# Sink heads: q produced in turned form, cosine and sine parts stacked to 128 rows of contraction

## The reference, cut to what matters

```python
def apply_rope(x, cos, sin):
    x1, x2 = jnp.split(xf, 2, axis=-1)
    return jnp.concatenate([x1 * c - x2 * s, x2 * c + x1 * s], axis=-1)

qa = apply_rope(qa.reshape(B, S, A_HEADS, A_HEAD_DIM), cos_a, sin_a)
ka = apply_rope(ka.reshape(B, S, A_KV_HEADS, A_HEAD_DIM), cos_a, sin_a)
y_a = swa_sink_attention(qa, ka, va, sinks)   # softmax(q k^T / 8, sink) v, bands of 2 chunks of 64 tokens
```

## Time and profile before

| | |
|---|---|
| runs | 763.81, 763.9, 764.29 us |
| profiled execution | 763.82 us, its span 762.1 us |
| granted TensorE clock | 0.998 of full |
| TensorE busy | 747.8 us, 98% of the span, 3970 matmuls |
| VectorE, ScalarE, GpSimd busy | 512.4, 417.0, 164.7 us |
| chain that ended last | TensorE 90%, VectorE 6%, ScalarE 2% |

### The profile page before, as it was taken

How to read it: one execution, slowest core, us unless ns; L and a number is a source line. 1 busy time by engine, 2 the same in 40 slices (tenths; PEclk the granted TensorE clock), 3 DMA queues, 4 the chain that set the end, 5 groups by cost and what they waited for, 6 DMA issues and landing times.

```text
span 762.1 us, 10863 instructions
## 1 busy us (share of the span) xinstructions
PE 747.8 (98%) x3970; PEld 631.5 (83%) x3970; DVE 512.4 (67%) x674; ACT 417.0 (55%) x789; POOL 164.7 (22%) x250
## 2 busy tenths in 40 slices
PE   6999999999999999999999999999999999999996
PEld 5978887888798888888888888788888988888885
DVE  5789867667765666656686887685568656565664
ACT  6847675534564444444577676654348444544452
POOL 1966422100131111100125443220002210111110
PEclk9999999999999999999999999999999999999999
DMA  7739533455465555566337493335463656564521
GB/s 256 254 99 299 186 111 111 151 182 171 158 201 186 193 193 171 163 216 207 104 103 257 174 304 111 111 111 168 164 220 111 221 166 221 176 209 171 202 68 55
DMA packets 68619, 132.16 MB, mean 173 GB/s; under 512 B 2874, under 2 KB 10596, under 8 KB 68324
## 3 DMA queue, kind: packets, MB, share of 16 engines
q1 hardware_dynamic: 68308, 131.64, 52.1%
q10 hardware_dynamic: 272, 0.00, 0.0%
HBM read 130.59 MB, written 1.05 MB: 173 GB/s over the span
## 4 chain that ended last, share of the span: by engine, by line
PE 90%; DVE 6%; ACT 2%; issue 1%; DMA 1%; POOL 0%; SPq 0%; POOLq 0%; ACTq 0%; DVEq 0%
PE acc L1353 18%; PE acc L1355 17%; PE acc L1354 17%; PE tp L1640 6%; PE sc L1640 6%; PE tp L1328 4%; PE sc L1435 3%; PE acc L1387 3%; PE tp L1642 3%; PE sc L1642 3%; DVE w_lo L995 2%; PE sc L1353 1%; PE sc L1354 1%; PE sc L1355 1%; DVE x L1160 1%; PE sc L1626 1%
## 5 line engine op out<-in xcount | busy, mean ns | idle before, releaser
L995 DVE TENSOR_TENSOR w_lo<-raw,w_hi 128x1024 fp32r<-128x1024 f32 (+3 forms) x256 | 307.9, 1222 | 163.0 <-ACT w_hi L654 161.4
L654 ACT CAST w_hi<-raw 128x1024 fp32r<-128x1024 f32 (+3 forms) x256 | 251.3, 996 | 181.1 <-PE acc L1355 107.9
L1353 PE MATMUL acc<-w_hi,s_hi 128*128 128x512 f32 (+1 forms) x328 | 127.7, 389 | 0.0
L1355 PE MATMUL acc<-w_hi,s_lo 128*128 128x512 f32 (+1 forms) x328 | 126.6, 386 | 0.0
L1354 PE MATMUL acc<-w_lo,s_hi 128*128 128x512 f32 (+1 forms) x328 | 126.5, 386 | 0.0
L1353 PE MATMUL acc<-w_hi,s_both 128*128 128x512 f32 (+2 forms) x320 | 122.0, 381 | 1.0 <-DVE w_lo L995 0.6
L1355 PE MATMUL acc<-w_hi,s_both 128*128 128x512 f32 (+2 forms) x320 | 118.5, 370 | 0.0
L1354 PE MATMUL acc<-w_lo,s_both 128*128 128x512 f32 (+2 forms) x320 | 118.4, 370 | 0.0
L517 POOL TENSOR_TENSOR tok<-k_b 128x512 f32<-128x512 f32 x32 | 36.9, 1159 | 266.0 <-ACT k_b L750 244.7
L1353 PEld LDWEIGHTS acc<-w_hi,s_hi 128*128 128x128 f32 x328 | 61.6, 188 | 13.1 <-DVE w_lo L995 1.3
L1355 PEld LDWEIGHTS acc<-w_hi,s_lo 128*128 128x128 f32 x328 | 61.6, 188 | 12.3
(11 more groups left out here) (186 smaller groups left out, 1076.0 us busy)
## 6 DMA issues: line engine op xcount, KB each, us to landing
raw<-in_w_mlp_in SPq DMA_DIRECT2D x32, 1024.0 KB, 5.4
raw<-in_w_mlp_out SPq DMA_DIRECT2D x32, 1024.0 KB, 5.0
raw<-in_w_in SPq DMA_DIRECT2D x24, 1024.0 KB, 5.4
raw<-in_w_oa SPq DMA_DIRECT2D x8, 1024.0 KB, 5.0
raw<-in_w_out SPq DMA_DIRECT2D x8, 1024.0 KB, 4.9
raw<-in_w_ob SPq DMA_DIRECT2D x4, 1024.0 KB, 5.0
raw<-in_w_in SPq DMA_DIRECT2D x3, 768.0 KB, 4.8
raw<-in_w_in SPq DMA_DIRECT2D x4, 576.0 KB, 6.5
```

Of the source, the lines that this page charges most:

```text
L654: s.copy(split_view(w_hi, p), raw_view(p)).then_inc(hi_ready, 1)
L995: v.tensor_tensor(split_view(w_lo, p), raw_view(p), split_view(w_hi, p).bitcast(F32), ALU.subtract)\
L1353: mm(banks[t][:, 0:N], h[:, kk, tk], wh[:, k, :], start=(start and k == 0), stop=False)
L1355: ins = mm(banks[t][:, 0:N], low[:, kk, tk], wh[:, k, :], start=False, stop=(stop and k == b - a - 1))
```

## The change

1. q of A comes out turned. A new `turned_product` (the former `mlp_in` with the banks as an argument) takes the weights as the stationary operand and the activations `s1` of all 256 tokens as the moving one: 24 matmuls of 256 columns for each piece in place of 12 of 512. Each bank then holds two blocks of [128 columns of q, 256 tokens].
2. The rotation is moved into the scores. For a head, q . rope = [q cos ; q sin] against [k' ; k' with its halves exchanged, one negated]. `qT_a` gets 128 rows: 64 of q times cosine, 64 of q times sine; `kT_a` gets 128 rows in two orders, for even and odd heads. The eight instructions for each group (`multiply_q`, four for each bank, 64 rows x 512 elements, PSUM times a table) are VectorE's.
3. The table is cosine and sine times 1/rms of the token (`scaled_cs`, four 128x128 instructions on GpSimd), turned by TensorE (new fill "angles", four blocks, ahead of "ckv") and copied by ScalarE (`turned_cs`, 128x512).
4. The products that next overwrite the banks of q now wait for VectorE: uq0 for `multiply_q` of group 0, uq1 for that of group 1, bank by bank (`q_taken`).
5. Gone: ScalarE's four copies of q to `tok`, the rotations of q on VectorE and GpSimd, the four turnings "qA" with their copies, GpSimd's clearing of the two extra rows. k of A is turned in one fill of four blocks (k' and the exchanged k') in place of two of one block, and copied by three instructions in place of four; GpSimd makes the exchanged halves with two small instructions for each token tile.

```diff
+            def multiply_q(pos, c, u):
+                src = acc[2 * (1 - c) + u][:, :].rearrange("p (x c q) -> p x c q", x=2, c=NCHUNK)
+                for odd in range(2):
+                    rows = slice(odd * AD, (odd + 1) * AD)
+                    for a in range(2):
+                        to = slice((a + odd) % 2 * AD, ((a + odd) % 2 + 1) * AD)
+                        table = turned_cs[rows, a]...to_broadcast([AD, 2, NCHUNK, CHUNK])
+                        ins = v.tensor_tensor(qT_a[to, c, :, odd, u]..., src[rows], table, ALU.mult)
+                ins.then_inc(q_multiplied, 1)
...
 # VectorE, behind lo(18), the key latent and neg_sink
-                dve.wait_ge(tables_ready, 1)
-                for c, p in ((0, 18), (1, 22)):
-                    lo(pos, p)
-                    dve.wait_ge(proj_out, pos.count(14, 2 * PROJ[f"q{c}"] + 1))
-                    rope(v, ..., between=lambda: lo(pos, p + 1)).then_inc(roped, 1)
-                    dve.wait_ge(roped, pos.count(2, c + 1))
-                lo(pos, 25)
-                turned(pos, ("qA", 0, 0))
-                lo(pos, 27)
-                turned(pos, ("qA", 0, 1))
+                dve.wait_ge(bank_done(("angles",)), bank_turn(pos, ("angles",)))
+                for c, p in ((0, 15), (1, 19)):
+                    lo(pos, p + 3)
+                    used(pos, p)
+                    multiply_q(pos, c, 0)
+                    lo(pos, p + 4)
+                    multiply_q(pos, c, 1)
...
 # TensorE
-                for i, p in enumerate(range(12, 16)):
-                    product(pos, p, 4 * (i // 2), s1, pair[1], i == 0, i == 3, free=latent_free(1) if i == 0 else None)
+                turned_product(pos, 12, pair[1], free=latent_free(1))
+                pe.wait_ge(angle_rows, pos.count(1, 1))
+                turn(pos, ("angles",), [scaled_cs[:, a, t]... for a in range(2) for t in range(TT)])
                 turn(pos, ("ckv",), ...)
-                for i, p in enumerate(range(16, 20)):
-                    product(pos, p, 4 * (i // 2), s1, pair[0], i == 0, i == 3, free=projected(pos, "kv") if i == 0 else None)
+                turned_product(pos, 16, pair[0], free=projected(pos, "kv"))
                 turned(pos, ("ckv",))
-                        for t in range(TT):
-                            turn(pos, ("kA", t), [k_a[:, t, :]])
-                    elif c < 3:
-                        pe.wait_ge(roped, pos.count(2, c))
-                        extra(pos, ("qA", 0, c - 1))
+                turn(pos, ("kA",), [k_a[:, t, g, :] for g in range(AKV) for t in range(TT)])
+                for c, (free, k0) in enumerate(((q_taken(0), 0), (q_taken(1), 0),
+                                                (projected(pos, "uq0"), KQ), (projected(pos, "uq1"), KQ))):
```

More of the change, by code:

```diff
@@ L110, in fill_order @@
     out = [("x", t, h) for t in range(TT) for h in range(2)]
-    out += [("cq", 0), ("cq", 1), ("ckv",), ("kA", 0), ("kA", 1), ("qA", 0, 0), ("qA", 0, 1)]
+    out += [("cq", 0), ("cq", 1), ("angles",), ("ckv",), ("kA",)]
     for r in range(NROUND):
@@ L683, in turned_copy @@
                 b = bank(name)
[L684 to L687, removed]
+                if name[0] == "angles":
+                    ins = s.copy(turned_cs, b[:, :].rearrange("p (a n) -> p a n", a=2))
+                elif name[0] == "kA":
+                    rows = b[:, :].rearrange("p (g n) -> p g n", g=AKV)
+                    s.copy(kT_a[:, 0], rows)
+                    s.copy(kT_a[0:AD, 1], rows[AD:P])
+                    ins = s.copy(kT_a[AD:P, 1], rows[0:AD])
                 else:
@@ L812, in _ @@
                 turned_hi(pos, ("cq", 1))
-                for c, p in ((0, 15), (1, 19)):
-                    hi(pos, p + 3)
-                    used(pos, p)
-                    for t in range(TT):
[L818 to L821, removed]
+                hi(pos, 18)
+                turned_copy(pos, ("angles",))
+                turned_hi(pos, ("ckv",))
+                hi(pos, 22)
                 for t in range(TT):
@@ L1411, in first_product, with turned_product @@
                     part(1, s1_lo, w_hi, [i], last=True, release=True)
+            def turned_product(pos, p, banks, free=None, between=None):
+                for i in range(4):
+                    if i == 2 and between is not None:
+                        between()
+                    pe.wait_ge(lo_ready, pos.count(NP, 2 * RAW + p + i + 1, 8))
+                    wh, wl = (split_view(w, p + i).rearrange("p (k n) -> p k n", k=2) for w in (w_hi, w_lo))
+                    for f in range(4):
+                        if i == 0 and f % 2 == 0 and free is not None:
+                            free(f // 2)
+                        out, cols = banks[f // 2][:, (f % 2) * SEQ:(f % 2 + 1) * SEQ], slice(f * P, (f + 1) * P)
+                        for k in range(2):
+                            kk = 2 * i + k
+                            mm(out, wh[:, k, cols], s1_hi[:, kk, :], start=(i == 0 and k == 0 and f % 2 == 0), stop=False)
+                            mm(out, wh[:, k, cols], s1_lo[:, kk, :], start=False, stop=False)
+                            ins = mm(out, wl[:, k, cols], s1_hi[:, kk, :], start=False, stop=(i == 3 and k == 1 and f % 2 == 1))
+                    ins.then_inc(piece_used, 1)
             def turn_h0(pos):
@@ L1545, in _ @@
-                for t in range(TT):
-                    turned(pos, ("kA", t))
-                for g in range(AKV):
-                    turned(pos, ("qA", 0, g))
+                pe.wait_ge(pool_roped, pos.count(6, 2 * POOL_ROPED["kA"] + 2))
+                turn(pos, ("kA",), [k_a[:, t, g, :] for g in range(AKV) for t in range(TT)])
+                for c, (free, k0) in enumerate(((q_taken(0), 0), (q_taken(1), 0),
+                                                (projected(pos, "uq0"), KQ), (projected(pos, "uq1"), KQ))):
+                    for i in range(2):
+                        product(pos, 20 + 2 * c + i, k0, s2, pair[1 - c % 2], i == 0, i == 1, free=free if i == 0 else None)
@@ L1549, in _ @@
+                turned(pos, ("kA",))
                 pe.wait_ge(consts_ready, CONST_STEPS)
```

140 lines of the change are left out of this document (55 added, 85 removed).

## The result

| | before | after |
|---|---|---|
| median | 763.97 us (14 runs) | 767.6 us (14 runs, 765.83 to 769.01) |
| ratio | | 1.0044, 95% interval 1.0035 to 1.0053 |
| profiled execution, its span | 763.82, 762.1 us | 768.3, 766.6 us |
| matmuls | 3970 | 4142 |

The kernel became 0.44% slower, some 3.4 us; the forecast was 766.3 us, 2.5 us slower than its profile of before. One run of before, at 1066 us, is left out of the ratio. The 14 times of after do not lie around their median. Seven are between 765.83 and 766.89 us (six of them at most 766.38), each with a granted clock of 0.999; seven are between 768.3 and 769.01 us, with 0.994 to 0.996. The median is the middle of the gap. The lower group, with a median of 766.1 us, is the forecast; the upper one, with a median of 768.8, has something that the forecast did not have at all. The profiled execution is of the upper group.

What follows compares the result with a forecast made beforehand. TensorE's stream plus its few holes bounds the kernel. Windows +2.35 us (layer 1) and +2.1 (layer 0), together +4.4, minus 2 x 0.98 behind them: +2.5 on 763.82, 766.3 us; range 763.6 to 769.0.

Steps and rivals of the forecast that it cites:

- Products: TensorE's q pieces: 96 matmuls of 256 columns, 11.6 us a group where it was 11.02; +2.4 us for four groups.
- the rival of half the distance of 512 columns: TensorE's 256-column matmuls at 0.115 us, not 0.120: 11.0 us a group, 765.1 us in all; chance 0.02.
- Turnings: TensorE: two of each layer's four qA turnings lie behind the window, in rounds 0 and 1; 0.98 us saved there.
- Scores of 128 rows: TensorE's scores: contraction growing from 66 to 128 rows changes nothing; scores of quantum 0 take about 1.0 us.
- VectorE's sequence: VectorE's multiplications, 0.70 us apart, hold uq1's second token tile: a new TensorE wait of 2.0 to 2.7 us a layer.
- the rival of 0.61: VectorE's multiplications 0.61 us apart, `neg_sink` at 0.35: 0.9 and 1.6 us less waiting, 763.8 us; chance 0.19.
- The hole of layer 0 ahead of piece 19: TensorE's 0.62 us idle until VectorE has split piece 19: closes, low part ready at 19.3 to 20.0, wanted at 21.0.
- `neg_sink` in layer 0: VectorE step ahead of the multiplications: 0.9 to 1.1 us beside GpSimd, ending at t = 16.0, against 15.3 in layer 1.
- After it 12 matmuls of 384 (2.2): TensorE behind the new wait: 12 matmuls of 384 columns take 2.2 us, to t = 32.8 or 33.5.
- the longer sequence: VectorE's multiplications at 0.75, `neg_sink` beside GpSimd in both layers, late probabilities: 2.7 us more, 769.0 us; chance 0.10.
- The rivals on the faster side: Overlapping multiplications 763.8 us (0.19), half-distance matmuls 765.1 us (0.02), no wait at all on VectorE 761.6 us (0.09).
- the forecast's two reasons for that: Multiplications not stretched by GpSimd: one input is in PSUM, and GpSimd's rotations of q, which ran here, are gone.

Runs made afterwards that it cites:

- the left-out half: The changed kernel without the sine parts of group 1 (two of each four multiplications left out), so it computes something else: 761.92 us, ratio 0.9969.
- the longer stretch: The changed kernel with two more VectorE copies of 512 elements ahead of group 1's last four multiplications, lengthening TensorE's wait: 772.72 us, ratio 1.0098.
- the short filler: The changed kernel with five filler matmuls on TensorE ahead of its wait for uq1's second token tile: 766.88 us, ratio 1.0036.
- the paired order: The changed kernel with each of group 1's bank 0 multiplications followed by bank 1's on the same rows, piece 23's low part ahead of all: 767.08 us once.

## Why the prediction came out as it did

**Products, as read.** 96 matmuls of 256 columns from 34.02 to the turning of the angles at 45.61: 11.59 us, forecast 11.6; the rival of half the distance of 512 columns had 11.0. The 109 ns per matmul of the Trainium skill, "TensorE: Matmul & The Clock Gate", section "Back-to-back issue gap", would have given 10.5; the section gives that formula for a matmul by itself and says that a stream with weight loads departs from it, and the trace departs from it upwards: 0.12 us each.

**Turnings, as read.** 1.03 us less behind each window, forecast 0.98. In rounds 0 and 1 nothing new waits; the probabilities of quantum 0 are turned straight behind the scores.

**Scores of 128 rows, as read but for 0.18 us.** The 24 of 64 columns take 81.88 - 79.20 = 2.68 us, the same as with 66 rows. The eight first ones of quantum 0 take 73.67 - 72.49 = 1.18 where the sum had "about 1.0"; no row had been read for them, though the trace of before had it: 71.38 - 70.19 = 1.19 us with 66 rows. Timeline of TensorE after:

```profile
72.49 1.05 PE L1449 MATMUL sc<-kT_a,qT_a 128*128 128x128 f32 x8
73.67 0.47 PE L1349 MATMUL acc<-w_hi,s_both 128*128 128x512 f32 x1
...
79.20 2.84 PE L1449 MATMUL sc<-kT_a,qT_a 128*128 128x64 f32 x24
81.88 0.60 PE L1324 MATMUL tp<-ident,probs 128*128 128x128 f32 x4
```

**VectorE's sequence, as read.** In t, from 34.02: key latent at 13.9 (forecast 13.9), multiplications from 15.3 (15.3), group 1 from 24.5 (24.4 to 25.1), the end at 30.7 (30.5 to 31.2), TensorE on at 30.8 (30.6 to 31.3). Their distance is 0.70, so the rival of 0.61 was wrong on this order of rows and right on the other. The hole of layer 0 ahead of piece 19 closed.

**`neg_sink` in layer 0, mis-sized.** 0.34 us in the timeline of VectorE above, forecast 1.1. The forecast had GpSimd still at work then; in the timeline of GpSimd it ends its work at 48.54, and `neg_sink` starts at 48.95. So TensorE goes on at t = 30.8 in both layers, not at 31.3 and 30.6. Put into the forecast's windows, with the 0.18 us of the scores: 40.0 - 0.5 + 0.18 = 39.68 and 39.3 + 0.2 + 0.18 = 39.68 us. Layer 0 measured 39.65, and layer 1's 41.22 less the 1.55 of lost clock is 39.67. Against the earlier trace rows that is 1.72 + 2.72, less 2 x 1.03: 2.4 us where the forecast had 2.5: 763.82 + 2.4 = 766.2 us, and the lower group has a median of 766.1 where the forecast had 766.3. The 0.57 us of the later start are not in this sum.

**The step that was missing: "After it 12 matmuls of 384 (2.2)".** This took the distance of matmuls from a stream that never stops and put it behind a hole that the same paragraph had just made. In layer 1 of the profiled execution they took 3.75 us, and half of all executions show the lower mean clock. In the earlier trace rows the clock is 1.00 with holes of at most 0.62 us inside; no row showed what it does after 2.0, so it was an unknown cost, and it should have been bounded from above like the others. With such a term the forecast would have been two values; the measured median, 767.6, lies between the groups only because the 14 executions fell half and half. The range took both groups in for another reason, the longer sequence on VectorE; that it holds them is in part luck. The rivals on the faster side fell by the waits and by the left-out half; the longer sequence did not occur, as the group of all multiplications shows (of VectorE in after, by form; busy time, mean ns, idle before):

```profile
L1067 DVE TENSOR_TENSOR qT_a<-acc,tok 64x512 f32<-64x512 f32 x32 | 22.0, 689 | 0.5
```

22.0 / 32 is 0.69 us each, and by tile they lie between 0.682 and 0.695, so none was stretched to the 1.70 of the earlier trace rows. (Those rows show two different steps; the same step L362 takes 1.70 us at 423.14 and 0.69 at 430.93.) Of the forecast's two reasons for that only one was put to the test: GpSimd had no work at all from 48.54 to 67.93, nor from 421.42 to 444.38, while the multiplications ran, so nothing here shows that an input in PSUM protects them.

What stays open: why the same hole loses the clock in one execution or layer and not in the next. The two profiled ones of the upper group lost 1.5 us each, in layer 1 only, while the medians of the groups lie 2.7 apart; both also had a late piece 12 (34.02 and 34.17 us, below), and what makes up the rest was not read. The executions at 0.994, of up to 769.4 us, may have lost the clock in both layers or, as with the longer stretch, for longer in one; none of those was profiled.

The 0.57 us by which piece 12 of layer 0 starts later are the start of the kernel, not the change. In the timeline of before the matmuls of 384 columns stand 0.32 us apart up to 11.55 and then 0.17, and twelve of them take 13.54 - 11.23 = 2.31 us; in after they stand 0.32 apart up to 12.90, and the same twelve take 14.12 - 10.98 = 3.14. From there to piece 12 both take 19.9 us (33.45 - 13.54 and 34.02 - 14.12). How long the engine stays slow there differs between executions: in the profiles of the other kernels here piece 12 starts between 33.45 and 34.17.

## What to carry to other kernels

When a change gives an idle stretch to an engine that is otherwise full, cost the work behind the stretch at both clocks. When a product moves from a bank that is quickly copied to one that is read by many instructions, ask first which bank is idle at that time, and put the low parts that the next product needs ahead of the readers whose bank no one wants yet: bank and order together were worth 5.3 us here (767.6 to 762.25, the lost clock included), more than the change itself, and the order alone 1.1 of them.

## What the runs showed of the hardware

- **The clock around a hole.** A hole in a full stream can cost TensorE half its clock for some microseconds, in some executions and not in others. Where it falls varies: 0.2 us after work began again (2.0 us hole, layer 1 of after), 1.1 us after it and 1.1 us before it (3.2 us hole, layers 0 and 1). Holes of 0.62 to 1.15 us never cost clock (the hole of 0.62 in the kernel before, 0.67 with uq1 in other banks, 1.15 with the short filler: 0.997 or more in each execution); 2.0 us did in 10 of 20 executions, 1.55 us in the layer that was profiled; 3.2 us did in 6 of 6. Longer is not always worse: two holes of 2.5 us kept it in the one execution of the paired order. Work that is thrown away kept the clock at no cost in time (windows from piece 12 to 28 of 39.66 and 39.64 us, 39.65 in layer 0 of after).
- **The clock column at the start.** From 9.70 to 10.98 us four matmuls of 384 columns of after stand 0.32 us apart, the distance of the low level, and the column says 1.00. So the holes of the first 8 us, of up to 2.6 us, are not counted above; and how long this slow start lasts makes 0.6 us between the profiles of before and after.
- **The held start of VectorE has a price.** 512 elements a row: 0.70 us from start to start with a change of rows (the multiplications of after), 0.60 (the paired order) to 0.61 (two copies) without.
- **More contraction rows cost nothing here.** With 66 or with 128 rows of contraction 24 scores of 64 columns take 2.68 us, and 8 of 128 columns 1.19 and 1.18 us.
